# Seven products in place of eight for row pairs 8 to 14 of a gate projection, with its weights loaded a pair ahead

## The reference

```
qa, ka, va, qr, kr, vr, gr, gate_a, gate_b = split(xn @ w_in)      # gr: 2048 wide, gate_a, gate_b: 1024 each
r = rms_plain(retention(qr, kr, vr)) * silu(gr)
a = rms_plain(diff_attention(qa, ka, va)) * subln_g * (1 - lam_init)
m = sigmoid(gate_a + ba) * (a @ w_pa) + sigmoid(gate_b + bb) * (r @ w_pb)
h = x + m @ w_o
y = rms_norm(h + (silu(g) * u) @ w_down)                           # g, u = split(rms_norm(h) @ w_gu)
```

## Time and profile before

| | |
|---|---|
| median of 3 runs | 2737.66 us (2736.84 to 2738.11) |
| the profiled execution: its own time | 2737.74 us |
| the profiled execution: its span | 2735.9 us |
| granted TensorE clock, mean | 0.999 of full speed |
| gates stage (first L2093 to last L2069) | 997 to 1595 us of the span |

### The profile page before, as it was taken

One profiled execution on the slowest core, in us unless ns is written; L12 is line 12 of the kernel. 1 busy time (PEld: TensorE's weight loads), 2 busy tenths in 40 slices (PEclk: granted clock), 3 DMA queues, 4 the chain that ended last, 5 costly groups with the idle time before them and its releaser, 6 DMA issues.

```text
span 2735.9 us, 41660 instructions
## 1 busy us (share of the span) xinstructions
PE 2706.7 (99%) x16114; PEld 2336.4 (85%) x16114; DVE 1380.2 (50%) x2760; ACT 732.6 (27%) x1549; POOL 867.9 (32%) x697
## 2 busy tenths in 40 slices
PE   8999999999999999999999999999999999999998
PEld 6888877777777779888888899999899999998887
DVE  6431355547777764666555533243485555542224
ACT  5111122225555532232222211011332222221012
POOL 2533423302211232221122235354124444455230
PEclk9999999999999999999999999999999999999999
DMA  4323356553343234456554554334122222245221
GB/s 161 112 101 132 107 193 207 196 180 116 99 134 110 101 130 164 159 192 198 188 193 146 194 185 145 126 120 159 47 82 72 77 90 72 72 150 176 85 61 66
DMA packets 277924, 362.15 MB, mean 132 GB/s; under 512 B 28530, under 2 KB 172530, under 8 KB 277746
## 3 DMA queue, kind: packets, MB, share of 16 engines
q1 hardware_dynamic: 277746, 359.74, 39.6%
HBM read 257.24 MB, written 111.35 MB: 135 GB/s over the span
## 4 chain that ended last, share of the span: by engine, by line
PE 95%; DVE 3%; issue 1%; ACT 1%; DMA 0%; POOL 0%; SPq 0%; DVEq 0%; ACTq 0%; POOLq 0%
PE psum L538 24%; PE psum L1354 14%; PE psum L2767 14%; PE psum L2093 12%; PE psum L563 10%; PE psum L1032 3%; PE psum L1057 2%; PE psum L2749 2%; PE psum L2142 2%; PE psum L2126 1%; PE psum L2791 1%; PE psum L1468 1%; PE psum L1044 1%; PE psum L2135 1%; PE psum L1008 1%
## 5 line engine op out<-in xcount | busy, mean ns | idle before, releaser
L364 POOL TENSOR_TENSOR w_h<-stage,ones 128x512 fp32r<-128x512 f32 x268 | 307.5, 1175 | 1297.2 <-PE psum L2093 387.1
L371 POOL TENSOR_TENSOR w_l<-stage,w_h 128x512 fp32r<-128x512 f32 x268 | 357.5, 1361 | 122.4 <-DVE acc L1185 117.7
L538 PE MATMUL psum<-w_h,xt_h 128*128 128x512 f32 x864 | 343.7, 398 | 3.2 <-POOL w_l L385 2.4
L538 PE MATMUL psum<-w_h,xt_l 128*128 128x512 f32 x864 | 341.9, 396 | 0.0
L538 PE MATMUL psum<-w_l,xt_h 128*128 128x512 f32 x864 | 341.9, 396 | 0.0
L2093 PE MATMUL psum<-xt_h,w_h 128*128 128x384 f32 x744 | 264.1, 355 | 0.1
L2093 PE MATMUL psum<-xt_l,w_h 128*128 128x384 f32 x744 | 244.8, 329 | 0.0
L2093 PE MATMUL psum<-xt_h,w_l 128*128 128x384 f32 x744 | 244.7, 329 | 0.0
L416 POOL TENSOR_TENSOR w_l<-stage,w_h 128x512 fp32r<-128x512 f32 x106 | 138.7, 1309 | 269.1 <-ACT w_h L2861 269.1
L1354 PE MATMUL psum<-w_h,xt_h 128*128 128x512 f32 x512 | 219.2, 428 | 0.0
L1354 PE MATMUL psum<-w_l,xt_h 128*128 128x512 f32 x512 | 202.2, 395 | 0.0
(11 more groups left out here) (308 smaller groups left out, 5723.8 us busy)
## 6 DMA issues: line engine op xcount, KB each, us to landing
stage<-in_w_in_dram SPq DMA_DIRECT2D x88, 512.0 KB, 5.8
proj<-edge SPq DMA_DIRECT2D x112, 256.0 KB, 2.0
stage<-in_w_gu_dram SPq DMA_DIRECT2D x88, 256.0 KB, 3.8
out_dram<-acc SPq DMA_DIRECT2D x43, 512.0 KB, 3.4
acc<-proj SPq DMA_DIRECT2D x82, 256.0 KB, 3.1
gates<-edge SPq DMA_DIRECT2D x32, 544.0 KB, 3.5
acc<-in_cache_k_dram SPq DMA_DIRECT2D x32, 512.0 KB, 5.8
acc<-in_cache_v_dram SPq DMA_DIRECT2D x32, 512.0 KB, 4.6
```

What stands on the lines that cost most here:

```text
L364: last = nc.gpsimd.tensor_tensor(w_h[s][:, a:b, :], src, one.unsqueeze(1).to_broadcast([128, b - a, WN]), ALU.mult)
L371: last = nc.gpsimd.tensor_tensor(w_l[s][:, a:b, :], stage[h][:, a - lo:b - lo, :], w_h[s][:, a:b, :].bitcast(F), ALU.subtract)
L538: last = nc.tensor.matmul(psum[:, bank, :], x, w[s][:, k, :], start=k == 0 and n == 0, stop=k == nk - 1 and n == len(passes) - 1)
```

## The change

**Rows in pairs.** The 32 rows become 16 pairs p of 48 groups y = 0 to 47. Weights come by the pair: two DMAs of 512 KB, 256 columns wide (before: four of 512 KB, 512 columns wide, for two pairs), and are split in four operands A11, A12, A21, A22 (row of the pair, half of the inputs). ACT makes the high part now (`gate_high`), GpSimd the low part (`gate_low`), both during the pair before.

**Pairs 0 to 7 and 15** compute as before, unit by unit.

**Pairs 8 to 14** use seven products of 128 x 512 by 512 x 320 on the two halves of the first 640 tokens, each product one unit of 4 groups, and the remaining 448 tokens as two plain units of 8 groups. The order is P1, PLAIN1, P2, PLAIN0, P6, P7, P4, P5, P3; each plain unit has two group numbers with nothing in them, so that the pair still has 48. GpSimd makes four sums of weight operands in place in `stage` (S3, S2, S1, S4). ACT copies each product out of its bank (`copy_out`), DVE adds the pieces in SBUF (seven additions of 320 columns for a pair), ACT applies the sigmoid. The finish of a pair falls in the first groups of the next one, and both of its rows are stored at y = 7 and y = 10 of it, from buffers that ACT writes again at y = 14 and y = 18.

**Sums of the tokens' halves**, T1 to T4, are made once, during pairs 0 to 3: in each, 8 additions and subtractions of 320 columns at y = 5 and 4 at y = 34 on DVE, 4 copies at y = 20 on ACT. They live in the part of w_h and w_l that five slots of operands leave free.

**The end of the stage.** W_PA is loaded at y = 6 of pair 15 and split by ACT and GpSimd, its block k = 4 after the last matmul of the gates, which has used that slot; before that copy ACT's order has the refills k = 5 and 6 of a_t. W_PA + 1 is loaded after the stage.

The core of the diff (count offsets for semaphores and the like are left out):

```diff
+GATE_FAST = range(GATE_PAIRS // 2, GATE_PAIRS - 1)
+GATE_OPS = {True: ("A11", "A12", "A21", "A22"), False: ("A11", "A21", "A22", "A12", "S2", "S3", "S1", "S4")}
+P1, PLAIN1, P2, PLAIN0, P6, P7, P4, P5, P3 = range(9)
+PRODUCTS = {P1: ("A11", "B11"), P2: ("A12", "B21"), P4: ("A22", "T4"), P7: ("S3", "T3"), P6: ("S2", "T2"),
+            P5: ("S1", "T1"), P3: ("S4", "B22")}
...
+    def load_gate_pair(sp, p):
+
+        if p < 2:
+            sp.wait_ge(w_split, split_count(W_FM - 1, 1))
+        else:
+            sp.wait_ge(op_split, gate_op(p - 1))
...
-        split_loop(16, 4)
...
+        for p in range(GATE_PAIRS):
+            if gate_plain(p):
+                for name in GATE_OPS[True]:
+                    gate_low(p, name)
+            else:
+                for name in ("A11", "A21"):
+                    gate_low(p, name)
+                gate_sum_made(p, "S3")
+                gate_low(p, "A22")
+                gate_sum_made(p, "S2")
+                gate_low(p, "A12")
+                gate_sum_made(p, "S1")
+                gate_sum_made(p, "S4")
+                for name in ("S2", "S3", "S1", "S4"):
+                    gate_low(p, name)
...
+        pool.wait_ge(gate_full, N_GATE_UNITS)
+        split(W_PA + 1, 1, no=tile_no(W_PA + 1), loaded=32 * (W_PA + 1))
...
-                    if x == 5 and row:
-                        store_gate(row - 1)
-                    if x == 16 and r == 1:
-                        load_w(sp, W_FM + row // 4 + 2)
+                    p, y = divmod(24 * row + x, 48)
+                    if gate_plain(p) and y == 29:
+                        store_gate(2 * p)
+                    if p and gate_plain(p - 1) and y == 5:
+                        store_gate(2 * p - 1)
+                    if p and not gate_plain(p - 1) and y == 7:
+                        store_gate(2 * p - 1)
+                    if p and not gate_plain(p - 1) and y == (7 if gate_plain(p) else 10):
+                        store_gate(2 * p - 2)
+                    if p + 2 < GATE_PAIRS and y == (11 if gate_plain(p) else 40):
+                        load_gate_pair(sp, p + 2)
+                    if p == GATE_PAIRS - 1 and y == 6:
+                        load_w(sp, W_PA)
...
+        def fast_pair(p):
...
+                    for k in range(4):
+                        sample_piece(2 * p + y // 24, y % 24)
+                        for n, (wt, low) in enumerate(((gop_h, False), (gop_h, True), (gop_l, False))):
+                            last = nc.tensor.matmul(psum[:, gate_bank(idx), 0:GH], wt(p, name)[:, k, :], gate_x(moving, k, low),
+                                                    start=k == 0 and n == 0, stop=k == 3 and n == 2)
...
+        def fast_steps(p, y):                                  # ACT
...
+            if y == 18:
+                act.wait_ge(gate_stored[0], 16 * (p + 1))
+                copy_out(p, P2, gate_part(2 * p, 0, GH))
+            if y == 26:
+                gated(p, "c11", 2 * p, 0, GH)
+            if y == 28:
+                wide_unit(2 * p, gate_unit(p, PLAIN0), GT, T - GT, None)
+            if y == 29:
+                gate_high(act, p, "S1")
+            if y == 30:
+                gate_high(act, p, "S4")
+            if y == 32:
+                copy_out(p, P6, part_gd)
+            if y == 33:
+                gate_high(act, p + 1, GATE_OPS[gate_plain(p + 1)][0])
+            if y == 36:
+                copy_out(p, P7, part_gc)
...
+        def plain_steps(p, y):                                 # ACT
...
+                if y == 13:
+                    gate_high(act, p + 1, GATE_OPS[gate_plain(p + 1)][0])
+                if y == 25:
+                    gate_high(act, p + 1, GATE_OPS[gate_plain(p + 1)][1])
+                if y == 26:
+                    gate_high(act, p + 1, GATE_OPS[gate_plain(p + 1)][2])
...
+            if k == PA_ORDER[-1]:
+                act.wait_ge(gate_full, N_GATE_UNITS)
...
             yield 24 * ROWS
+            merge_high(PA_ORDER[-1])
             for c in range(3):
-                unit(3 * ROWS - 3 + c)
+                plain_unit(GATE_PAIRS - 1, 3 + c)
...
+        def fast_steps(p, y):                                  # DVE
...
+            if y == 22:
+                dve.wait_ge(gate_read, gate_unit(p, P2) + 1)
+                add(gate_part(2 * p, 0, GH), b)
+            if y == 35:
+                dve.wait_ge(gate_read, gate_unit(p, P6) + 1)
+                add(b, d)
+            if y == 39:
+                dve.wait_ge(gate_read, gate_unit(p, P7) + 1)
+                dve.wait_ge(v_done, gate_step(p, "u2"))
+                add(c, b)
+            if y == 43:
...
+                add(row1_a, c)
+            if y == 47:
+                dve.wait_ge(gate_read, gate_unit(p, P5) + 1)
+                add(b, row1_b)
+                add(row1_b, c)
...
+                    if y == 2 and p and not gate_plain(p - 1):
+                        last_sum(p - 1)
```

More of the change, by code:

```diff
@@ L553, in pe_feature_tile @@
                     pe.wait_ge(bank_free, count + 3)
+            if j == 1 and holder is not None:
+                pe.wait_ge(*holder)
             for k in range(KD):
@@ L1853, in store_gate @@
             s = row % 2
-            sp.wait_ge(gate_ready, row + 1)
+            sp.wait_ge(gate_ready, row + 1 if gate_plain(row // 2) else row // 2 * 2 + 2 - s)
             sp.dma_start(gates[row * 128:(row + 1) * 128, :], edge[:, s * T:(s + 1) * T]).then_inc(gate_stored[s], 16)
@@ new lines, in wide_group @@
+        def wide_group(p, r, k, idx, a, width):
+            name = (("A11", "A12"), ("A21", "A22"))[r][k // 4]
+            if k % 4 == 0:
+                pe.wait_ge(op_split, gate_op(p, name) + 1)
+            for n, (wt, x) in enumerate(((gop_h, xt_h1), (gop_h, xt_l1), (gop_l, xt_h1))):
+                last = nc.tensor.matmul(psum[:, gate_bank(idx), 0:width], wt(p, name)[:, k % 4, :], x[:, k, a:a + width],
+                                        start=k == 0 and n == 0, stop=k == KD - 1 and n == 2)
+            if k == KD - 1:
+                last.then_inc(gate_full, 1)
```

432 lines of the change are left out of this document (333 added, 99 removed).

## The result

The changed kernel takes 2750.75 us (median of 5 runs, 2748.21 to 2752.7) against 2736.84 us: a ratio of 1.0050, 95% interval 1.0035 to 1.0065. It is slower by 13.9 us where 5.9 us less were forecast. The profiled execution took 2750.62 us, its span is 2748.8 us, 12.9 us above that of before.

A forecast was written before the change was run, and what follows sets the result against it. PE's own work was taken to bound the kernel, with only DVE ever late. The terms -12.4 + 6.4 - 2.4 + 1.0 + 1.5 = -5.9 us took the median 2737.66 to 2731.8 us; 8-in-10 range 2725 to 2741.

The forecast's parts named there:

- What PE saves: Matmuls of pairs 8 to 14: seven products save 1.78 us a pair, -12.4 us in all, with 5% fewer matmul columns.
- rival D: DVE becomes the bound from y = 29 to 50 of every seven-product pair: +9.4 us, 2747; chance 19%.
- The form of the sum: Whole kernel: savings and waits simply added up, -5.9 us in all, with no term for a slower clock.
- SP, stores and loads: Weight loads have 36 us to land in 5.8 and row stores hold nothing up: 0, bound up to 1 us a pair.
- ACT: In the products ACT's 1.66 us of work just fits PE's 1.76 us per unit: 0, else 0.1 to 1 us a unit.
- if PE waited on ACT's copies: Sign that the forecast is wrong: PE waiting in the products on ACT's copies of product banks.
- What DVE gets: Additions and slower DVE work beside GpSimd in pairs 8 to 14 make PE wait: +6.4 us, between 0 and some 20.
- The price of an addition beside GpSimd: DVE's additions of 320 columns: 0.49 us alone, some 0.54 us more beside GpSimd, about 1.03 us.
- Taken away: DVE's waits in whole-tile splits go, at 1155 and 1460 us: -2.4 us, between 0 and -4.
- Sums of token halves: Eight DVE instructions at y = 5 of pairs 0 to 3 delay pair 3's quads: +1.0 us, between 0 and 4.
- The end: W_PA's block k = 4, copied behind refill k = 6, makes the merge wait: +1.5 us, between 0 and 3.

The follow-up runs named there:

- placed_plain: placed2 with no seven-product pair (pairs 8 to 14 unit by unit) and the loads of two pairs at other marks: 2733.8 us.
- placed3: placed2 with two of pair 10's additions behind the quad's adds and the last block's token-half sums made in pair 4, not 3: 2719.4 us.
- no_adds: Changed kernel with DVE's seven additions in each of pairs 8 to 14 replaced by their semaphore counts alone: 2742.7 us.
- spread_loads: Changed kernel with stores and reloads of state issued later, between loads of values, and pair weight loads at other marks: 2741.4 us.
- end_root: Changed kernel with refills k = 5 and 6 behind W_PA's block k = 4 and the last head's root behind pair 14's first quad: 2741.7 us.
- all_plain: Changed kernel with no seven-product pair, pairs 8 to 14 computed unit by unit, the rest of the change kept: 2745.2 us.
- placed2: Changed kernel with spread_loads' transfers, W_PA's k = 4 ahead of the refills, later roots behind quads, one-input root, some additions of pairs 11 and 12 moved: 2727.3 us.
- long_waits: Kernel before with nine memsets put ahead of DVE's `normalise` in four chunks whose quads wait for it: 2768.5 us.
- moved_all_loads: Changed kernel with pair weight loads issued just behind loads of values and stores of state 7 groups later, reloads moving along: 2765.0 us.
- root_one_after: Changed kernel with end_root's edits and the root chain's instruction in its one-tensor-input form: 2740.1 us against 2741.7.
- placed: Changed kernel with moved_all_loads' transfers, W_PA's k = 4 ahead of the refills, later roots behind quads and many additions moved: 2758.9 us.
- short_waits: Kernel before with three memsets ahead of `normalise` in seven chunks whose quads wait for it: 14.7 us more span.

## Why the prediction was wrong

**What PE saves**, -12.4: right. 0.204 us for 448 columns, and 12.1 us between placed_plain and placed3. Two slips beside it enter no sum: these pairs have 7.4% fewer matmul columns (48384 for 52224) and not 5%, and rival D's conditions, 2.1 and 2.9 us a pair, leave out the 2.5 us that its own price holds; with them they are 1.8 and 2.5.

**The form of the sum** failed first: every wait was entered at its own length. The clock was read as full in the earlier trace rows, and the one drop behind the wait of 1.1 us at 1096 us, which lay inside a mean of 0.99, was not looked for. The span came out 18.8 us above the forecast (12.9 more than before, not 5.9 less): 9.4 us are the half clock, 8.0 are waits (14.5 more than before, where the sum had 6.5), and 1.4 the ledger does not find.

**SP, stores and loads**, 0, and **ACT**, 0: failed, and they are nearly all of the 8.0 us of waits. "Loads of weights have a pair of 36 us to land and cost nothing" asked when the load is needed and not what is queued behind it. "It just fits" counted ACT's own work, 1.66 us of 1.76, and not its waits for others: 5.0 us for the values, and at 1447 us `keys_low`, which stands behind an addition (no_adds takes that wait away). These gave PE 2.7 + 0.5 us at 1196, 2.4 at 1347, 1.4 at 1447 and 0.4 at 1514, 7.4 us in all; spread_loads, which took the first three away, gave 9.3 back (with the luck told there). A sign of it stood in the earlier trace rows: ACT was idle for 17.5 us behind the loads of values in the kernel before, and none of it reached PE. In the changed kernel it is 16.9 us, but 5.0 and 4.6 of it come at two places where PE's next operand or bank is queued behind. The stores of rows did as forecast: ACT waited 9.1 us for them, and none of PE's waits stands behind one. The text had named "if PE waited on ACT's copies" as what would make it wrong.

**What DVE gets**, +6.4: the waits of the fast pairs on DVE are 8.3 us (0.56, 0.36, 1.45, 0.94, 4.99), where 8.2 were forecast with pair 14's own 1.8. That the sum fits is luck. Pair 8 came out at 0.9 for 1.0, pair 10 at 1.45 for 2.0, pair 12 at 0.94 for 1.0 (but by its last addition, ahead of pair 13's quad), pair 14 at 3.2 above its former wait for 1.5. Of these only the waits of pairs 8 and 12, 1.9 us, go with the additions (no_adds). Pair 10's goes with GpSimd's sums. In pair 14 it was the sample's root, which was not in the text, and `normalise` behind it: they met GpSimd three times. In time the additions cost 8 us and the sums 3.5, since half clock followed.

**The price of an addition beside GpSimd** was taken too low, 0.54 us on top of 0.49. Of the 49 additions in the changed kernel, 25 met no instruction of GpSimd and took 0.47 to 0.49 us; the 24 that met one took 1.56 us in the median and 1.59 at most, 1.1 more. The rule of the Trainium skill that the prediction names (SBUF — State Buffer, Who interferes with whom: VectorE and GpSimd share a port and the loser waits out the other's instruction) speaks for such a price. The trace agrees, with at most 1.1 us added beside instructions of 1.29 us (median), and the one-input form at a steady 0.28 us shows what it is that gets held.

**Taken away**, -2.4: 3.9 went, inside its bounds; the waits at 1155 and 1460 us are gone (2.4), and so are those of 1.27 at 1293 and 0.19 at 1310 us, which were not counted. **Sums of token halves**, +1.0: 1.15 us (1.59 + 0.67 at pair 3's quads against 1.11). **The end**, +1.5: 3.2 us, double, and 6.8 us of half clock with it. The path was right: from the merge's start refill k = 6 begins 5.7 us later and not 4.4, since both refills waited longer for their loads (4.0 and 1.4 us for 3.0 and 1.0; why they came later was not followed), and the block's low part took 1.85 us and not 1.35. end_root gave 9.0 us back for both its places.

So the time is nearest to rival D's, 2747 for 2750.8, by another mechanism: DVE never became the bound (placed3 has it as busy, without the waits), and 3.2 us of the 14.5 us of added waits went with the additions.

What stays open: why a wait is followed by half clock in one place and not in another (pair 14's quad: 1.83 us in all_plain, yes; 1.82 us in the kernel before, no). The 1 to 2.5 us by which some runs miss the ledger were not followed up, nor was each of placed2's moves run alone. A load of values issued before the chunk's second `update` was not tried, since its buffer is still read then.

## What to carry to other kernels

Where PE is over 98% busy, read the granted clock in stretches of a few microseconds at each of its waits, and price a wait of 2 us or more at its length and some 2 us on top (long_waits: 5.2 us of wait, 7.8 of time); several small moves that each remove one wait are then worth more than they look, and one late instruction costs more. A transfer that has plenty of time is not free: list what is issued behind it on its queue, which engine waits for that in order, and what stands behind that wait. After a cure, look at the next use of the same buffer or adds, for the wait may only have moved; it did in moved_all_loads, root_one_after and placed.

## What was not expected of the hardware

Half clock came in stretches of 3.4 or 6.8 us, once 10.2 (no_adds, at the wait of 4.99 us). It began 2.3 us after the end of a wait of 1.1 us in the kernel before, and already during the waits of 4.8 to 5.5 us. Equal waits were not equal: 1.31 us was followed by 3.4 us of it in placed3, 1.50 us by none in short_waits. A one-column instruction of VectorE took 0.23 us alone and up to 1.18 us beside GpSimd (1.37 in the changed kernel) with two SBUF tensor inputs, and 0.28 us always with one tensor input and two per-partition scalars.
